# Linear attention of block 2: one factor tile a level, token-major outputs, output gates as wide groups

## The reference

```python
# gla_mixer, per head, chunks of 64 tokens
log_a = log_sigmoid(gate_lr @ gate_w2 + gate_b) / 16.0
b = cumsum(log_a)                                   # within the chunk
o_inter = (q * 128**-0.5 * exp(b)) @ state
decay = exp(where(causal, b[t] - b[s], -inf))       # per channel d
scores = einsum('td,sd,tsd->ts', q * 128**-0.5, k, decay)
o = o_inter + scores @ v                            # state carries the chunks before
out = rms_norm(o, norm_g) * silu(out_gate)          # the root is over the 256 values of a head
# hybrid_layer
h = x + concatenate([gla_out, nsa_out]) @ w_out
```

## Time and profile before

| | |
|---|---|
| runs | 2802.87, 2802.89, 2808.12 us |
| the profiled execution's own time | 2805.94 us |
| its span in the trace | 2803.8 us |
| its mean granted TensorE clock | 0.987 of full speed |
| PE busy | 2707.3 us, 97% of the span |
| DVE, ACT, POOL busy | 1197.2, 1212.0, 1179.4 us |

### The profile page before, as it was taken

The page is one execution under the profiler, slowest core; times in us unless marked ns, Lnnn a source line. Parts: engine busy times, 40 slices in busy tenths (PEclk is TensorE's granted clock), DMA queues, the critical chain, the costliest instruction groups (busy, mean ns, idle before and its releaser), DMA issues.

```text
span 2803.8 us, 34630 instructions
## 1 busy us (share of the span) xinstructions
PE 2707.3 (97%) x14176; PEld 2319.1 (83%) x14176; DVE 1197.2 (43%) x1500; ACT 1212.0 (43%) x1446; POOL 1179.4 (42%) x530
## 2 busy tenths in 40 slices
PE   7999889999999999999999978999999999999999
PEld 7999777778888888888888878989788888888887
DVE  6998744443432222222332577555532232222222
ACT  5333335444454444444444444435454444444333
POOL 3556544334444444444444333323244444444443
PEclk9999999999999999999999989999999999999999
DMA  6444435355555555555555533344355555555554
GB/s 227 161 143 170 145 130 173 135 206 185 191 185 189 187 195 183 192 188 194 197 196 189 175 110 117 135 167 137 116 176 199 185 194 186 190 193 183 202 203 150
DMA packets 72445, 489.05 MB, mean 174 GB/s; under 512 B 8363, under 2 KB 10060, under 8 KB 14688
## 3 DMA queue, kind: packets, MB, share of 16 engines
q1 hardware_dynamic: 72288, 486.84, 50.5%
HBM read 484.71 MB, written 2.10 MB: 174 GB/s over the span
## 4 chain that ended last, share of the span: by engine, by line
PE 84%; DVE 8%; issue 3%; ACT 2%; POOL 1%; DMA 0%; SPq 0%; DVEq 0%; ACTq 0%; POOLq 0%
PE PB L578 22%; PE PB L582 22%; PE PB L579 22%; PE PB L546 3%; PE PB L550 3%; PE PB L547 3%; ACT WH L1133 1%; PE PB L596 1%; DVE TM L2321 1%; DVE WL L1611 1%; DVE TM L2318 1%; POOL WL L2420 1%; DVE TM L1654 1%; PE PB L1088 1%; DVE TM L1662 0%
## 5 line engine op out<-in xcount | busy, mean ns | idle before, releaser
L2420 POOL TENSOR_TENSOR WL<-RAW,WH 128x1024 fp32r<-128x1024 f32 x442 | 1078.7, 2441 | 1502.6 <-ACT WH L1133 1502.6
L1133 ACT ACTIVATE WH<-RAW 128x1024 fp32r<-128x1024 f32 x892 | 941.8, 1059 | 1251.0 <-PE PB L582 1092.0
L1611 DVE TENSOR_TENSOR WL<-RAW,WH 128x1024 fp32r<-128x1024 f32 x450 | 580.2, 1290 | 1442.2 <-ACT WH L1133 1442.1
L578 PE MATMUL PB<-WH,HNH 128*128 128x512 f32 x1792 | 703.0, 392 | 7.1 <-DVE MIX L2256 4.6
L582 PE MATMUL PB<-WL,HNH 128*128 128x512 f32 x1792 | 699.0, 390 | 7.5 <-POOL WL L2420 7.5
L579 PE MATMUL PB<-WH,HNL 128*128 128x512 f32 x1792 | 698.0, 390 | 0.0
L578 PEld LDWEIGHTS PB<-WH,HNH 128*128 128x128 f32 x1792 | 336.9, 188 | 80.9 <-DVE MIX L2256 5.8
L582 PEld LDWEIGHTS PB<-WL,HNH 128*128 128x128 f32 x1792 | 336.6, 188 | 80.1 <-POOL WL L2420 9.7
L546 PE MATMUL PB<-HNH,WH 128*128 128x256 f32 x1312 | 386.0, 294 | 9.7 <-ACT WH L1133 9.7
L579 PEld LDWEIGHTS PB<-WH,HNL 128*128 128x128 f32 x1792 | 336.9, 188 | 68.7
L550 PE MATMUL PB<-HNH,WL 128*128 128x256 f32 x1312 | 377.6, 288 | 14.1 <-DVE WL L1611 9.8
(11 more groups left out here) (348 smaller groups left out, 2216.6 us busy)
## 6 DMA issues: line engine op xcount, KB each, us to landing
RAW<-in_w_gu SPq DMA_DIRECT2D x176, 1024.0 KB, 4.8
RAW<-in_w_dn SPq DMA_DIRECT2D x88, 1024.0 KB, 4.8
RAW<-in_w_in_a SPq DMA_DIRECT2D x57, 1024.0 KB, 4.9
RAW<-in_w_in SPq DMA_DIRECT2D x45, 1024.0 KB, 4.9
RAW<-in_w_out SPq DMA_DIRECT2D x32, 1024.0 KB, 4.9
RAW<-in_w_ga SPq DMA_DIRECT2D x24, 1024.0 KB, 4.8
RAW<-in_w_gb SPq DMA_DIRECT2D x24, 1024.0 KB, 4.8
WIN<-in_win SPq DMA_DIRECT2D x8, 512.0 KB, 5.6
```

Of the source, the lines that this page charges most:

```text
L578: e.matmul(o, hi[:, k, x], WH[:, s, c], start=k == 0, stop=False)
L1133: e.activation(WH[:, u % NSPL, :], RAW[:, n % NRAW, half * SU * 128:(half + 1) * SU * 128], ACT.Copy).then_inc(*wt.act.mark(("wh", u)))
L1611: e.tensor_tensor(WL[:, u % NSPL, :], RAW[:, n % NRAW, half * SU * 128:(half + 1) * SU * 128], f32(WH[:, u % NSPL, :]), ALU.subtract).then ...
L2420: e.tensor_tensor(WL[:, u % NSPL, :], RAW[:, n % NRAW, half * SU * 128:(half + 1) * SU * 128], f32(WH[:, u % NSPL, :]), ALU.subtract).then ...
```

## The change

- **Levels.** One tile GE[lv % 3] of three holds both factors: DVE multiplies its half by GK (`keys`), POOL the other half by GQ (`queries`), and PE multiplies the tile with itself. A level takes one step instead of four; on DVE `before(lv)` is at step lv+3, `keys(lv)` at lv+4, `taken(lv)` at lv+6, and PE's level at lv+5. The scale 1/16 goes into exp, 128^-0.5 into the squares and the root. Level 7's exponents take 3 instructions on DVE, 1 on POOL and 3 exps on ACT.
- **Rate.** 1.3/16 instead of 2.2/16 of a step a tile; 3.4/16 instead of 3.3/16 for the sparse attention.
- **og and vs** are `group`s (the weights are packed for it): 2 groups of 64 tiles and 1 of 64. ACT reads their banks and scales by RTOK (SiLU for og).
- **Outputs** have tokens as rows (two fp32 matmuls moving 256 columns a value half, three a head), ACT squares with accumulation per token, one root and one reciprocal serve all heads, DVE gates (`gated`), ACT scales (`z`), PE transposes 4 squares a head (`mg`), ACT and DVE split.
- **v rows** are turned two rows later, inside the row (tile 8 on PE, tile 12 on DVE).
- POS, CW2 and CM are loaded with the other constants before row c.

```diff
-        SECOND = (("v", 8, 16), ("og", 8, 16), ("ks", 4, 16), ("kc", 4, 16), ("vs", 2, 32), ("cmp", 2, 32),
-                  ("nq", 8, 16), ("mg", 4, 32))
+        SECOND = (("v", 8, 16), ("og", 2, 64), ("ks", 4, 16), ("kc", 4, 16), ("vs", 1, 64),
+                  ("cmp", 2, 32), ("nq", 8, 16), ("mg", 4, 32))
...
-            w.beside(second(w, gla(), nsa()), 2.2)
+            w.beside(second(w, gla_steps(w), nsa_steps(w)), 1.3)
```

PE:

```diff
-                for lv in range(7):
-                    ke, qe = KE2[lv % 2], QE2[lv % 2]
-                    bb = [wide_bank("level", lv, 0), wide_bank("level", lv, 1)]
+                for lv in range(8):
+                    x = GE[lv % 3]
+                    bb = [wide_bank("level", lv, c) for c in range(2 if lv < 7 else 1)]
                     e.wait_ge(*gl.dve.done("k", lv))
+                    e.wait_ge(*gl.pool.done("q", lv))
+                    for c, b in enumerate(bb):
+                        for h in range(4):
+                            s = slice(c * 128, (c + 1) * 128)
+                            t = e.matmul(b[:, h * 128:(h + 1) * 128], x[:, h, s], x[:, h, s if lv < 7 else slice(128, T)],
+                                         start=True, stop=True)
...
+                    e.matmul(bank[:, 0:T], PT[:, 0, h, :], VTG[:, 0, v], start=True, stop=True)
+                    e.matmul(bank[:, T:2 * T], PT2[:, h, :], VTG[:, 0, v], start=True, stop=False)
+                    e.matmul(bank[:, T:2 * T], PT[:, 1, h, :], VTG[:, 1, v], start=False, stop=True).then_inc(
+                        *gl.pe.mark(("out", h)))
...
                     if name == "vs":
-                        npair(nt)
+                        group(nt, HNH, HNL, 16)
+                    elif name == "og":
+                        group(NT["og"] + 2 * j, HNH, HNL, 16, None, {} if j else {1: values_turned, 2: gates_turned})
...
-                        tile_row(nt)
-                        if name == "v" and j:
-                            v_turned(j - 1)
+                        tile_row(nt, 16, None, {8: lambda: v_turned(j - 2)} if name == "v" and j > 1 else {})
```

DVE (one call of each a step) and POOL:

```diff
+                def before(lv):
+                    if lv >= 3:
+                        e.wait_ge(*gl.pe.done("level", lv - 3))
...
+                        e.tensor_tensor(x[:, :, 0, :], end, g[:, :, 0, :], ALU.subtract).then_inc(*d.mark(("a", lv)))
-                    e.tensor_tensor(qe, flat(GQ[:, :, :]), ge, ALU.mult).then_inc(*d.mark())
-                    e.tensor_tensor(ke, flat(GK[:, :, :]), ge, ALU.mult).then_inc(*d.mark(("k", lv)))
+                def keys(lv):
+                    e.wait_ge(*gl.act.done("e", lv))
...
+                    e.tensor_tensor(x, k, x, ALU.mult).then_inc(*d.mark(("k", lv)))
...
+                before(0)
+                yield
+                for lv in range(1, 8):
+                    keys(lv - 1)
+                    before(lv)
+                    if lv >= 3:
+                        taken(lv - 3)
+                    yield
+                keys(7)
+                taken(5)
+                yield
+                taken(6)
...
+                def queries(lv):
+                    e.wait_ge(*gl.act.done("e", lv))
...
+                    e.tensor_tensor(x, q, x, ALU.mult).then_inc(*gl.pool.mark(("q", lv)))
...
+                for lv in range(1, 8):
+                    queries(lv - 1)
+                    after(lv)
+                    yield
+                queries(7)
```

ACT:

```diff
+                    if name == "og":
+                        for h in range(2):
+                            nt = NT["og"] + 2 * j + h
+                            e.wait_ge(*wt.pe.done("nt", nt))
+                            e.activation(OG[:, h, columns(j)], mb(nt)[:, 0:512], ACT.Silu,
+                                         scale=RTOK[:, h:h + 1]).then_inc(*m.act.mark(("og", j, h), ("free", nt)))
...
+                    for c in range(2):
+                        e.activation(ST[:, c, :], bank("out", h)[:, c * T:(c + 1) * T], ACT.Square, scale=128.0 ** -0.5,
+                                     accum_out=OS[:, h, c:c + 1]).then_inc(*gl.act.mark(*([("osq", h)] if c else [])))
```

More of the change, by code:

```diff
@@ L437, in mlstm @@
                     yield
[L439 to L453, removed]
             e.dma_start(VEC[:, :], A["vecs"]).then_inc(landed["vec"], 16)
@@ L607, in turn_hidden @@
                 turn(("z", stage), SIG, j, lambda h: e.wait_ge(*m.dve.done("z", stage, j, h)))
[L609 to L628, removed]
             def hn_ready(stage):
@@ L1252, in gla @@
             def gla():
[L1253 to L1261 removed]
+                ge = flat(GE[0][:, :, :])
                 e.wait_ge(*gl.dve.done("abs"))
@@ new lines, in gla @@
+                for h in range(4):
+                    e.wait_ge(*gl.dve.done("z", h))
+                    for c in range(2):
+                        z = GP[:, c, 256 * h:256 * h + 256]
+                        e.activation(z, z, ACT.Copy, scale=OR[:, h, c:c + 1]).then_inc(
+                            *gl.act.mark(*([("z", h)] if c else [])))
+                yield
+                yield
+                for h in range(4):
+                    turned(h)
+                    if h % 2:
+                        yield
@@ new lines, in gated, with turned @@
+                    e.wait_ge(*gl.act.done("osq", h))
+                    for c in range(2):
+                        v = slice(256 * h, 256 * h + 256)
+                        e.wait_ge(*m.act.done("og", h // 2, c))
+                        e.tensor_tensor(GP[:, c, v], bank("out", h)[:, c * T:(c + 1) * T], OG[:, c, v],
+                                        ALU.mult).then_inc(*d.mark(*([("z", h), frees("out", h)] if c else [])))
+                def turned(h):
+                    e.wait_ge(*gl.act.done("mg", h))
@@ L2368, in vector @@
                     nt = NT[name] + j
-                    run(of)
+                    for k in tiles(of):
+                        if name == "v" and j > 1 and k == 12:
+                            v_turned(j - 2)
+                        if name == "og" and j == 0 and k in (22, 24):
+                            v_turned(6 if k == 22 else 7)
+                        if name == "og" and j == 0 and k == 40:
+                            e.wait_ge(*m.pe.done("gate"))
+                            e.tensor_copy(flat(GATE[:, :, :]), bank("gate")[:, 0:48]).then_inc(
+                                *m.dve.mark("gate", frees("gate")))
                     if name == "v":
```

441 lines of the change are left out of this document (185 added, 256 removed).

## The result

The changed kernel takes **2784.31 us**, the median of 4 runs (2782.24 to 2787.73), beside 2802.88 us for the kernel before in the same comparison (2802.17 to 2808.12). The ratio is 0.9931, with a 95% interval of 0.9914 to 0.9948. So it is faster by 18.6 us, and the forecast was 28.4 us. The profiled execution took 2787.73 us with a span of 2785.5; the span of before was 2803.8, so 18.3 us are to be found in the trace.

What follows compares the result with a forecast made beforehand. PE, busy 97% of the span, was taken as the bound, though DVE feeds the rows of v. Terms -3.6 - 1.8 - 13.4 - 4.6 - 5.0 = -28.4 us gave 2777.5, less 3.05: 2774.5 us, range 2754 to 2793.

Steps and rivals of the forecast that it cites:

- The groups: og and vs as groups of 512-column matmuls: og -2.4 us, vs -1.2, together -3.6 us.
- The wait in vs: vs: normalisations and CB come earlier, so PE's 5.6 us wait for DVE's low half goes: -5.0 us.
- The gate: Gate in the rows of v: step 1 at tile 13 instead of 8, so PE waits less: -1.8 us.
- The clock: Levels 1 and 7 no longer follow an idle PE at the low clock: 1.8, 0.9 and 1.9, together -4.6 us.
- The levels: Waits of PE at levels and turned v rows: 16.5 us instead of 29.9, so -13.4 us.
- The walk: Tracing the in-order queues from the start of v: waits of 8.5, 1.5 and 6.5 us, v ending at 1714.1.
- The rest: Remaining parts, among them `nsa` at rate 3.4 instead of 3.3: 0, within 1 us either way for `nsa`.
- Rival 1: Rows of v: nothing waits but the gate; 16.5 us and about 4 us of clock go too: 2754, chance 0.15.
- Rival 2: v rows: convolution, SiLU, WH and low half form a ring, +10 us; CB's delay stays, +5: 2789.5, chance 0.15.
- Rival 3: v rows: the same ring with POOL's port claims in series, 20.2 us a row: 2813.5, slower, chance 0.06.
- Rival 4: Each level's wait moves to another place and og only swaps widths: 2799, chance 0.05.

Runs made afterwards that it cites:

- run 6: Changed kernel with one empty step more between linear and sparse attention, so `nsa` starts one step later: 2784.78 us.
- Run 3: Changed kernel with POOL's eight low halves of the v rows cut to 8 of 1024 columns: 2767.73 us.
- second execution: The changed kernel run again, nothing changed, to see whether its waits return: 2782.30 us.
- Run 2: Changed kernel with all sparse-attention steps 4 tiles (0.85 of a step) later: 2778.82 us, ratio 0.9901 to the kernel before.
- run 4: Changed kernel with a copy in place of SiLU in the v rows, so no table changes there: 2787.02 us.
- run 9: Changed kernel with every low half of the v rows on DVE, none on POOL: 2767.41 us.
- run 11: Changed kernel with low halves of c and v rows and both level products on DVE, sparse-attention steps 4 tiles later: 2761.68 us.
- run 12: Changed kernel with low halves of c and v rows on DVE and sparse-attention steps 4 tiles later; POOL keeps its level product: 2760.01 us.
- run 5: Changed kernel with linear-attention steps every 17.8 tiles up to step 12, then every 8: 2788.30 us, ratio 0.9937 to the kernel before.
- run 8: Changed kernel with PE taking each level one step (12.3 tiles) later, DVE as it is: 2786.03 us.

## Why the prediction was right in direction and too large by 10 us

The time lies inside the stated range, 2754 to 2793, and 9.8 us above the forecast of 2774.5. The misses have both signs: 4.2 us too little in the rows of c and v, 5.3 for cmp and nq, 1.9 each for the start and mg, 0.9 for og, against 4.1 that ks, kc and vs gave beyond the forecast. That these last gave more was not foreseen and hides a part of the error.

**The groups (-3.6): held.** vs was put at 21.8 us of matmuls and takes 21.91. The matmuls of 512 columns stand 0.2275 us apart, as in the earlier trace rows.

**The wait in vs (-5.0): held.** The wait is gone, and run 6 brings it back with 5.83 us by one step alone. With the clock, which was 0.89 there and is 1.00, vs gained 9.0: 1.2 of width, 5.6 of waiting, and the rest, 2.2, beside the clock's rise.

**The gate (-1.8): held.** 4.7 became 2.90 us.

**og, ks and kc.** og gained 12.5 us where 13.4 were forecast; the wait of 1.8 before its turned v row was not in the forecast. ks and kc gained 13.8 us: the 6.1 before level 7, its two clock terms (2.8) and the 3.6 of side work that now stands in og make 12.5. og, ks, kc and vs together gained 35.2, and the forecast has 32.1 for them. Of the 3.1 more, 2.2 are those of vs, the rest was not separated; the granted clock of 1.00 in all three windows, where it was 0.95, 0.92 and 0.89, stands beside it.

**The clock (-4.6): held for level 7, not in the rows of v.** Level 1 takes 1.95 us, but level 2, which took 2.02 before, takes 3.62 after its new wait, so what the one gave the other took back.

**The levels (-13.4): mis-sized, -10.0.** The walk put 16.5 us of waits in the rows of v; 19.9 are there if the turn in og (1.8) is counted. Level 0, forecast 8.5, took 8.46 and the turn at tile 104, forecast 6.5, took 6.07. For level 0 both ends of the wait stand 3.2 us later than in the walk (1660.8 for 1657.5, 1669.2 for 1666), 1.9 of it by the later start. Level 3 took 0.76 for 1.5. What I missed are level 2 (2.57), where I had said that levels 1 and 2 find their factors, since the masked copy was late with its bank, and the turn in og (1.8). With small ones beside them and the clock behind each, c and v became 7.9 us longer where 3.7 were forecast. I had weighed the port against a whole stretch ("if nothing but the port paced the levels, v would end near 1710") and kept the walk. Run 3 shows that the walk had the right waits but had not priced how much of them was POOL: of the 86.3 us, 14.7 hang on eight low halves of POOL (1.8 of them come back in og). That is no error of the sum, but it was the largest gain that the runs found.

**The rest ("0 within 1 us either way"): this step failed.** Changing 3.3 to 3.4 and the number of steps before it moved the whole `nsa` part against the tiles. The step behind cmp came at tile 1 of nq instead of tile 5, before ACT had made HIDT, and PE stood 4.9 us (2.6 in the second execution), then ran at the lower clock: the window has 0.96 where it had 1.00, +5.3 us. In the second execution cmp with nq is 2.3 us longer than before the change, and with waits of 2.2 to 3.1 us in six more runs that is the likelier size; the rest of the 5.3 belongs to the profiled execution. Run 2 undoes it with 0.85 of a step: cmp with nq falls to 77.8 us. I had counted the steps and not where each would fall. mg's +1.9 goes with waits of the same part (PC, 1.70 and 2.63 for 1.40 and 1.59), and in the second execution it is only +0.6; I did not separate it.

**The start (+1.9)** is before any line of the change but its three small loads; over all runs the first c row starts between 1562.5 and 1567.1. It belongs to this pair of executions.

**The rivals.** Rival 1 (only the gate waits) fell: level 0 waits as forecast. Rival 2 (a ring through SiLU and tables) came near in its time, 2789.5, but not in its mechanism: run 4 takes the table loads away and gains 0.9 us in this stretch, and CB's delay, the other half of that rival, did not stay. The other parts of its ring were not taken away singly. Rival 3 did not come, though its cause, POOL's claims in series, is the one that run 3 finds large. Rival 4 (waits only move) fell: 29.9 us of waits became 19.9, though what `nsa` lost in vs it got back in part behind cmp.

**What stays open:** how the 7 us before level 0 that remain with the low halves moved to DVE (runs 9, 11, 12) divide. The timeline of run 9 shows that they pass in DVE's own queue, after the exp has ended and before the keys. In run 3, where those low halves were on neither engine, 2.1 us remained. No run took a scan, a convolution or an exponent out of that queue.

## What to carry to other kernels

When two engines share a port, price an operation by what it blocks, not by whose queue it is in: a low half takes 2.4 us on POOL, during which DVE was held up here, and 1.2 on DVE itself, so giving DVE *more* work made it finish earlier. When steps are spread over tiles by a rate, a change of the rate or of the count moves every later step against its producers: list for each the tile at which it falls and what it needs there, before writing "0". And give each wait its partner: look where the step that frees a bank stands before the turn that takes it. Spreading the levels (run 5) or giving DVE another step (run 8) only moved the waits to the turns. No run moved the turns alone.

## What was not expected of the hardware

- The blocking reaches DVE's scans (674 to 1728 ns) and not only products of two tiles. The scaling of one tile by a column, from which the prediction had taken it, goes from 354 ns to 2.04 us; the masked copy from PSUM kept its 719 to 730 ns.
- A convolution of 1.52 us took 5.13 us while POOL ran three operations back to back. In the next row, where POOL ran the same three, it took 3.10.
- A wait of 8.46 us before level 0 cost a second time, as before: 3.73 us instead of 1.95 for the same 16 matmuls. Between gate and og the granted clock was 0.86 where PE was idle for 86.3 - 67.0 = 19.3 us, and 0.93 in run 11, where it was idle for 12.9.
- Eleven table loads of 1.28 us less on ACT, 14 us, were worth 0.9 us between gate and og, and og took 2.4 longer (run 4): ACT is busy for 47 of the 86 us there and idle for 22.4 before its SiLUs (L1564), which wait for DVE's convolution.
